# Gate products moved into the state-space groups, two multiplications left on GpSimd

## The chip, the cores and the metric

The kernel runs on one NeuronCore of one Trainium2 chip. The metric is the device time of one execution in microseconds, 2592.23 us in the median of three runs before the change (2590.69 to 2595.5).

## The reference, cut to what matters

The program is two transformer blocks in float32 on 256 tokens, the second with 256 more tokens of context. The change touches only the Mamba-2 mixer of the second block: 512 tokens (context and sequence, four tiles of 128), 8 groups of 4 heads, state size 128.

```python
z, xbc, dtr = split(u @ in_w)                 # z: 2048 gate columns = 16 chunks of 128
xbc = silu(dwconv(xbc) + b)                   # x (16 chunks of 128), B (8), C (8)
cb = einsum(C, B);  seg = exp(min(acum_l - acum_s, ...)) * tri
y_diag = einsum(cb * seg, x * dt)             # per group of 4 heads
y_off  = einsum(C, h_prev, exp(acum))
y = y_f + flip(y_b) + D * x
out = rmsnorm(y * silu(z), norm_w) @ out_w
```

## The kernel before

The mixer starts about 735 us into the execution and ends at 1318 us. Each engine has one instruction stream, written out in program order; a semaphore wait stops all that stands behind it on that engine. All activations are kept transposed, one chunk being 128 channels by 512 tokens.

**Weights** come in "halves" of 128 x 2048 (1 MB, two chunks of eight contraction tiles). Three slots hold raw halves, two hold the high parts. For each half ScalarE makes the high part (`round_half`, line 1768), VectorE the low part in place (`lower_half`, line 1773, which raises `w_split`), and TensorE multiplies three times for each pair of tiles (`matmul_split`, lines 464 to 466): 24 matmuls of 128x512 a chunk (`product`, line 1776). `product` waits for `w_split` to reach the number of its half, so it also waits for every half before it. The load of half w waits for half w-3 to be used, its rounding for half w-2. The order of halves before is 16 for x, B and C (two a group), 8 for z, 8 for the output projection.

**The group loop** runs over g = 0 to 7. TensorE in group g: chunk 0 of the next group; the C·B products and the transposes to token order (`to_tokens`, lines 1812 and 1818); chunks 1 and 2 of the next group; the states (line 1828); chunk 3; then `outputs` (line 1852), which waits for `m_ready` of both directions. Where there is no next group (g = 7), gate chunks 0 to 3 stand in those four places (`following`).

VectorE in group g: mask the C·B bank (line 2219), convolve chunk 0 of the next group (line 2114, four instructions), clip both directions of the decay rows (line 2230), mask_decay(0) (line 2236), convolve chunk 1, combine states (2249 to 2255), mask_decay(1), one `lower_half`, convolve chunks 2 and 3, add the output banks to `Yt` (line 2272), one more `lower_half`. ScalarE takes the banks out, makes the exponentials `cea` (lines 2068 to 2071, which release the clips) and the 32 decay exponentials (line 2007), and applies silu. GpSimd multiplies inputs by their weights (line 1960) and `cea` by C (line 1967); these are "the two multiplications" of the title, and they stay where they are.

**After the loop** TensorE makes gate chunks 4 to 15 (`gate`), with `sum_squares` of four chunks at a time (line 1906) between them, then the gate banks of `g1` (line 1688), the last sum and its transposition ("sst", line 1921), and the output projection: 8 halves of 48 matmuls of 128x512 into all eight PSUM banks. ScalarE applies silu to each gate bank (`gated`), squares (`square`) and rounds y; VectorE multiplies y by the gate (`use_gate`, line 2124) and makes the low part of y (`lower_y`, line 2129).

PSUM is a ring of eight banks in order of opening: a bank may be written when the one eight before it is emptied. After the mixer come the expert layers, whose weight loads wait for the last output bank.

## Time and profile before

| | |
|---|---|
| median of 3 runs | 2592.23 us (2590.69 to 2595.5) |
| the profiled execution | 2590.05 us |
| its span, first to last instruction | 2588.2 us (1.85 us lie around it) |
| TensorE / VectorE / ScalarE / GpSimd busy | 84% / 44% / 25% / 7% of the span |
| mean granted TensorE clock | 0.929 |
| mixer's group loop, first C·B mask to the end of the last outputs | 794.1 to 1147.9 us |
| after the loop, to the last matmul of the projection | 1147.9 to 1316.4 us |

Times are microseconds from the start of the span; "x8" is a count of instructions merged in one row, whose second number is then the time from the first's start to the last's end. "[3.33 <-PE bank L1812]" is idle time of the engine before the row, and what ended it. PE is TensorE, PEld its weight loads, DVE is VectorE, ACT is ScalarE, POOL is GpSimd. A clock of 1.00 is 2.4 GHz, 0.50 is 1.2 GHz.

### The profile page before, as it was taken

How to read it: one execution, taken by the hardware profiler on the slowest of the kernel's cores; microseconds unless marked ns; L12 is line 12 of the kernel's file. 1: busy time of each engine (PE TensorE's matmuls, PEld its weight loads, DVE VectorE, ACT ScalarE, POOL GpSimd, SP SyncE). 2: the span in 40 equal slices, each digit the busy share in tenths (PEclk: the TensorE clock that was granted, in tenths of full speed). 3: DMA queues.
4: the chain of work that ended last, by engine and by line, in shares of the span. 5: the costliest groups of instructions: out<-in, count | busy, mean ns of one | idle time of the engine just before them, and what ended most of it. 6: DMA issues, size and time to landing. Idle time of an engine off the chain costs nothing. (4 is left out here: it accounts for less than half of the span.)

```text
span 2588.2 us, 27436 instructions
## 1 busy us (share of the span) xinstructions
PE 2165.1 (84%) x10982; PEld 1296.4 (50%) x10982; DVE 1130.1 (44%) x1520; ACT 654.0 (25%) x1197; POOL 179.8 (7%) x103
## 2 busy tenths in 40 slices
PE   7975988999968868699968988888787879888886
PEld 5743455999957767577854322222343443222222
DVE  4566235777658888864141222212327421111112
ACT  4232132000036766654111111111104211111110
POOL 0000000000003524420000000000000000000000
PEclk9968988999979989899979999999898979999998
DMA  8735184555324223222243999999920129999997
GB/s 302 257 120 198 65 308 148 179 194 190 118 56 129 82 82 114 82 82 82 82 195 139 427 428 428 429 428 429 405 98 1 47 95 428 429 429 428 428 428 295
DMA packets 171348, 600.81 MB, mean 232 GB/s; under 512 B 14307, under 2 KB 97638, under 8 KB 144646
## 3 DMA queue, kind: packets, MB, share of 16 engines
q1 hardware_dynamic: 166640, 579.62, 57.2%
q0 software_dynamic: 2352, 16.91, 1.7%
q10 hardware_dynamic: 2278, 3.20, 0.4%
q8 instruction: 54, 0.88, 0.1%
q14 instruction: 24, 0.20, 0.0%
HBM read 598.53 MB, written 1.18 MB: 232 GB/s over the span
## 5 line engine op out<-in xcount | busy, mean ns | idle before, releaser
L2523 PE MATMUL bank<-slots,hT 128*64 128x512 f32 x3072 | 694.5, 599 | 119.9 <-DMA slots<-in_moe_w 87.2
L2523 PEld LDWEIGHTS bank<-slots,hT 128*64 128x64 f32 x3072 | 209.4, 137 | 558.9 <-issue 376.5
L464 PE MATMUL bank<-hT_r,slots_r 128*128 128x256 f32 (+1 forms) x896 | 299.0, 334 | 1.2 <-DVE slots_r L460 1.2
L2603 DVE TENSOR_TENSOR hT<-hT,bank 128x512 f32<-128x512 f32 x32 | 22.0, 688 | 527.0 <-PE bank L2523 527.0
L465 PE MATMUL bank<-slots_r 128*128 128x512 f32 x512 | 200.8, 392 | 0.0
L464 PEld LDWEIGHTS bank<-hT_r,slots_r 128*128 128x128 f32 x896 | 170.6, 190 | 20.9 <-issue 3.9
L330 POOL TENSOR_SCALAR rstd<-eps_rows 128x2 f32<-128x2 f32 (+4 forms) x16 | 3.9, 243 | 2145.8 <-ACT xn L396 683.1
L466 PE MATMUL bank<-slots_r 128*128 128x512 f32 x384 | 150.0, 391 | 0.0
L465 PE MATMUL bank<-hT_r,slots_r 128*128 128x256 f32 x512 | 144.8, 283 | 0.0
L466 PE MATMUL bank<-hT_r,slots_r 128*128 128x256 f32 x512 | 144.8, 283 | 0.0
L528 PE MATMUL bank<-slots,hT 128*128 128x512 f32 (+1 forms) x320 | 131.5, 572 | 4.0 <-ACT hT L445 2.7
L2584 ACT ACTIVATE hT<-bank 128x512 f32<-128x512 f32 x32 | 19.1, 597 | 450.5 <-PE bank L2523 450.5
L2114 DVE SCALAR_TENSOR_TENSOR slots<-slots,vcols 128x512 f32<-128x512 f32 x128 | 123.8, 972 | 13.4 <-ACT slots L1988 9.7
L2607 DVE TENSOR_TENSOR xne<-bank,xne 128x512 f32<-128x512 f32 x32 | 22.1, 692 | 222.6 <-PE bank L2523 222.6
L1852 PE MATMUL bank<-rowsB,slots 128*64 128x128 f32 x512 | 46.9, 341 | 78.7 <-DVE rowsB L2236 72.4
L460 DVE TENSOR_TENSOR slots_r<-slots,slots_r 128x4096 fp32r<-128x4096 f32 (+1 forms) x32 | 107.5, 3359 | 1.1
L465 PEld LDWEIGHTS bank<-slots_r 128*128 128x128 f32 x512 | 97.3, 190 | 19.5
L1967 POOL TENSOR_TENSOR slots<-slots 128x1536 f32<-128x1536 f32 (+2 forms) x24 | 105.8, 4432 | 0.0
L1773 DVE TENSOR_TENSOR slots_r<-slots,slots_r 128x2048 fp32r<-128x2048 f32 x32 | 73.2, 2287 | 69.7 <-ACT slots_r L1768 69.5
L2588 ACT ACTIVATE hT<-bank 128x512 f32<-128x512 f32 x32 | 19.1, 597 | 324.4 <-PE bank L2557 324.4
L465 PEld LDWEIGHTS bank<-hT_r,slots_r 128*128 128x128 f32 x512 | 98.1, 192 | 0.6
L466 PEld LDWEIGHTS bank<-hT_r,slots_r 128*128 128x128 f32 x512 | 98.1, 192 | 0.0
(457 smaller groups left out, 3299.2 us busy)
## 6 DMA issues: line engine op xcount, KB each, us to landing
slots<-in_moe_w SPq DMA_DIRECT2D x192, 2048.0 KB, 25.5
slots<-in_ada_w SPq DMA_DIRECT2D x24, 2048.0 KB, 11.6
slots<-in_ssd_in_w SPq DMA_DIRECT2D x48, 512.0 KB, 5.3
slots<-in_moe_w_gate SPq DMA_DIRECT2D x16, 1024.0 KB, 5.5
slots<-in_moe_w_up SPq DMA_DIRECT2D x16, 1024.0 KB, 8.0
slots<-in_moe_w_down SPq DMA_DIRECT2D x16, 1024.0 KB, 5.4
rowsB<-acum_rows POOLq DMA_DIRECT2D x16, 1024.0 KB, 6.4
slots<-in_w_in SPq DMA_DIRECT2D x7, 2048.0 KB, 17.9
```

Source lines behind the costliest of these rows:

```text
L460: return dve.tensor_tensor(low, x, high.bitcast(F32), ALU.subtract)
L464: pe.matmul(out, lhsT[0], rhs[1], start=start, stop=False, skip_group_check=True)
L465: pe.matmul(out, lhsT[0], rhs[0], start=False, stop=False, skip_group_check=True)
L466: return pe.matmul(out, lhsT[1], rhs[0], start=False, stop=stop, skip_group_check=True)
L528: i = pe.matmul(b.ap[:, 0:width], lhsT(k), rhs(k), start=(k == 0), stop=(k == K - 1))
L1773: dve.tensor_tensor(low_half(w), raw_half(w), high_half(w).bitcast(F32), ALU.subtract).then_inc(w_split, 1)
L1852: i = pe.matmul(pair[h // 2].ap[64 * j:64 * j + 64, tt], left, right, start=(at == 0), stop=(at == len(terms) - 1), tile_position=(0, 64 * ...
L1967: i = pool.tensor_tensor(cea[:, d, :, to:to + n], cea[:, d, :, to:to + n], conv[:, 3, at:at + n].unsqueeze(1).broadcast_to([P, HPG, n]), A ...
L2114: i = dve.scalar_tensor_tensor(o, padded[:, c, :, j:j + S], tap(j, CH(g)[c]), o, ALU.mult, ALU.add)
L2523: i = pe.matmul(bank[64 * n:64 * n + 64, :], lhsT(4 * h + k), wv[:, k, n * 512:(n + 1) * 512], start=(h == 0 and k == 0), stop=(h == 1 and ...
L2603: dve.tensor_tensor(acts, sg, psum[1][:, :], ALU.mult).then_inc(a_ready, 1)
L2607: dve.tensor_tensor(ye[j], psum[3][:, :], g2, ALU.mult).then_inc(ye_ready, 1)
```

## The change

Twelve of the sixteen gate chunks are made inside the groups. The order of halves becomes A0 B0 A1 B1, then A_g B_g Z_(g-2) for g = 2 to 7, then Z6 Z7 and the eight O (A: x, B: B and C, Z: gate, O: output projection). In groups 1 to 6 TensorE makes gate chunks 2g-2 and 2g-1 between chunk 3 and `outputs`; in group 7 the four places hold chunks 12 to 15; none is left after the loop. `sum_squares` takes two chunks at a time, and stands before `to_tokens` in groups 2 to 7 and twice after the loop. `round_half` and `lower_half` are called three times a group in the order of the halves; the clips now stand before the convolution of chunk 0. ScalarE and VectorE make silu, product and square of the two chunks in the same group. The high part of y is rounded after the loop, in the time of the projection; the transposition of the sums uses the last output bank. Buffers: gate values lie in the two last chunks of `Yt` until they are needed, `y_high` partly in `h_high`, `ssum` in `w_dt`. Nothing on GpSimd's queue changes. The diff, cut:

```diff
@@ -279,16 +279,17 @@
...
+        HALVES = [("A", 0), ("B", 0), ("A", 1), ("B", 1)]
+        for g in range(2, SSD_G):
+            HALVES += [("A", g), ("B", g), ("Z", g - 2)]
+        HALVES += [("Z", 6), ("Z", 7)] + [("O", q) for q in range(8)]
...
                         project(g + 1, c)
                     else:
-                        gate(c)
+                        gate(12 + c)
+
+                def sum_squares(q):
+
+                    pe.wait_ge(y_squared, 2 * q + 2)
+                    b = banks.open(("ss", q), DVE)
+                    pe.wait_ge(*b.emptied)
+                    for j in range(2):
+                        i = pe.matmul(b.ap[64 * j:64 * j + 64, :], const("ones")[:, 0:64], gate_buf(2 * q + j), start=True,
+                                      stop=True, tile_position=(0, 64 * j), skip_group_check=True)
...
@@ -1890,48 +1906,41 @@
                 project(0, 3)
                 for g in range(SSD_G):
                     following(g, 0)
+                    if g >= 2:
+                        sum_squares(g - 2)
                     to_tokens(g)
                     following(g, 1)
                     following(g, 2)
                     states(g)
                     following(g, 3)
+                    if 1 <= g < SSD_G - 1:
+                        gate(2 * g - 2)
+                        gate(2 * g - 1)
                     outputs(g)
 
-                def sum_squares(q):
-
...
@@ -2011,17 +2018,26 @@
 
                     b = banks["z", i]
                     act.wait_ge(bank_full, b.full)
-                    if i >= 2:
-                        act.wait_ge(z_used, i - 1)
-                    act.activation(sz[:, i % 2, :], b.ap[:, :], ACT.Silu).then_inc(emptied[ACTE], 1)
+                    if 2 <= i < 12:
+                        act.wait_ge(bank_full, banks["ss", i // 2 - 1].full)
+                    elif i >= 12:
+                        act.wait_ge(conv_done, 4 * SSD_G)
+                    act.activation(gate_buf(i), b.ap[:, :], ACT.Silu).then_inc(emptied[ACTE], 1)
 
                 def square(i):
 
                     act.wait_ge(z_used, i + 1)
-                    if i >= 4 and i % 4 == 0:
-                        act.wait_ge(bank_full, banks["ss", i // 4 - 1].full)
-                    act.activation(squares[:, i % 4, :], Yt[:, i, :], ACT.Square).then_inc(y_squared, 1)
-                    act.activation(y_high[:, i, :], Yt[:, i, :], ACT.Identity, scale=y_gain(i)).then_inc(y_rounded, 1)
+                    act.activation(gate_buf(i), Yt[:, i, :], ACT.Square).then_inc(y_squared, 1)
...
@@ -2054,52 +2070,66 @@
                     more = g + 1 < SSD_G
                     smooth(g, 3)
                     if more:
+                        if g:
+                            round_half(act, B_HALF(g + 1))
                         take(g + 1, 0)
                     else:
-                        gated(0)
+                        round_half(act, Z_HALF(7))
+                        gated(12)
                     for t in range(TT):
                         copy_out(act, ACTE, ("tok", g, t), tok[:, t, :], 384)
...
                     if more:
                         take(g + 1, 1)
                     decay(g, 1)
-                    if not more:
-                        gated(1)
-                    round_half(act, 2 * g + 4)
                     if more:
+                        if g:
+                            round_half(act, Z_HALF(g - 1))
                         smooth(g + 1, 0)
                         take(g + 1, 2)
                         smooth(g + 1, 1)
                         take(g + 1, 3)
+                        if g + 2 < SSD_G:
+                            round_half(act, A_HALF(g + 2))
+                        else:
+                            round_half(act, Z_HALF(6))
                         smooth(g + 1, 2)
+                        if g:
+                            for i in (2 * g - 2, 2 * g - 1):
+                                gated(i)
+                            for i in (2 * g - 2, 2 * g - 1):
+                                square(i)
                     else:
...
-                        gated(3)
-                    round_half(act, 2 * g + 5)
-                act.wait_ge(bank_full, banks["y", SSD_G - 1, 1].full)
-                for i in range(3):
-                    square(i)
-                for i in range(4, 16):
-                    gated(i)
-                    square(i - 1)
-                    if i % 2:
-                        round_half(act, 18 + i // 2)
+                        skip(g, 0)
...
                 square(15)
                 for s_ in range(2):
                     for n in range(2):
                         copy_out(act, ACTE, ("g1", s_, n), g1[:, s_, n * 512:(n + 1) * 512], 512)
-                for w in range(26, 32):
-                    round_half(act, w)
+                act.wait_ge(bank_full, banks["y", SSD_G - 1, 1].full)
+                for q in range(2, 8):
+                    round_y(2 * q - 2)
+                    round_y(2 * q - 1)
+                    round_half(act, OUT_HALF(q))
...
@@ -2219,28 +2284,20 @@
                         i = dve.tensor_tensor(cbm[:, d, :].rearrange("p (t n) -> p t n", t=TT),
                                               b.ap[:, :].rearrange("p (t n) -> p t n", t=TT), mask, ALU.mult)
                     i.then_inc(emptied[DVE], 1)
+                    if more and g:
+                        lower_half(dve, B_HALF(g + 1))
+                    elif not more:
+                        lower_half(dve, Z_HALF(7))
+                    clip(g, 0)
+                    clip(g, 1)
                     if more:
                         convolve(g + 1, 0)
...
-                        use_gate(0)
...
-                                          ALU.mult).then_inc(m_ready, 1)
-
-                    mask_decay(0)
+                        use_gate(12)
+                    dve.wait_ge(emptied[DVE], banks["cbs", g].done)
+                    mask_decay(g, 0)
                     if more:
...
@@ -2256,51 +2313,41 @@
                         i.then_inc(emptied[DVE], 1)
                         dve.wait_ge(emptied[DVE], b.done)
                     dve.sem_inc(hp_ready, 1)
-                    mask_decay(1)
-                    lower_half(dve, 2 * g + 4)
+                    mask_decay(g, 1)
                     if more:
+                        if g:
+                            lower_half(dve, Z_HALF(g - 1))
                         convolve(g + 1, 2)
+                        lower_half(dve, A_HALF(g + 2) if g + 2 < SSD_G else Z_HALF(6))
                         convolve(g + 1, 3)
+                        if g:
+                            use_gate(2 * g - 2)
+                            use_gate(2 * g - 1)
                     else:
-                        use_gate(2)
-                        use_gate(3)
-                    for c in range(2):
-                        b = banks["y", g, c]
-                        dve.wait_ge(bank_full, b.full)
...
+                        use_gate(13)
+                        lower_half(dve, OUT_HALF(0))
+                        lower_half(dve, OUT_HALF(1))
+                        lower_y(0)
+                        lower_y(1)
+                    add_output(g)
+                use_gate(14)
+                use_gate(15)
+                sum_batch(6)
+                sum_batch(7)
+                lower_y(2)
+                lower_y(3)
+                b = banks["so", TT - 1, 1]
+                dve.wait_ge(sst_full, 1)
+                dve.tensor_scalar(eps_rows[:, 0:TT], b.ap[:, 0:TT], 1.0 / 64, None, ALU.mult).then_inc(sst_taken, 1)
+                dve.wait_ge(sst_taken, 1)
+                dve.sem_inc(y_summed, 1)
+                for q in range(2, 8):
+                    lower_half(dve, OUT_HALF(q))
+                    if q < 7:
+                        lower_y(2 * q)
+                        lower_y(2 * q + 1)
                 lower_y(14)
                 lower_y(15)
-                sum_batch(3)
```

The helper `clip`, `mask_decay` and `add_output` hold the instructions of before; `skip` is the D·x product taken out of `smooth`.

## Rows read from the trace of the kernel before

**Rows 1.** Busy time by stretch: us, PE, PEld, DVE, ACT, POOL, clock, DMA.

```profile
950.00:1000.00 50.00, 36.70 (x247) 31.44 (x246) 44.47 (x37) 33.23 (x67) 20.99 (x9) 0.90 0.30 93
1150.00:1200.00 50.00, 50.00 (x227) 39.54 (x226) 23.74 (x25) 23.15 (x32) 0.00 (x0) 1.00 0.30 84
```

**Rows 2.** Costliest groups, page part 5: busy, mean ns, idle before, releaser.

```profile
L1852 PE MATMUL bank<-rowsB,slots 128*64 128x128 f32 x512 | 46.9, 341 | 78.7 <-DVE rowsB L2236 72.4
```

**Rows 3.** VectorE in group 4, in order of time: start, us, instruction.

```profile
976.83 1.29 DVE L2219 TENSOR_TENSOR slots<-bank,consts 128x512 f32<-128x512 f32 x2 [3.33 <-PE bank L1812]
979.49 5.04 DVE L2114 SCALAR_TENSOR_TENSOR slots<-slots,vcols 128x512 f32<-128x512 f32 x4 [1.37 <-ACT slots L1988]
984.45 8.20 DVE L2230 TENSOR_TENSOR rowsB<-rowsB,slots 128x2048 f32<-128x2048 f32 x2
992.57 3.38 DVE L2236 TENSOR_TENSOR rowsB<-rowsB,slots 128x2048 f32<-128x2048 f32 x1
995.88 5.22 DVE L2114 SCALAR_TENSOR_TENSOR slots<-slots,vcols 128x512 f32<-128x512 f32 x4
...
1004.88 2.29 DVE L2236 TENSOR_TENSOR rowsB<-rowsB,slots 128x2048 f32<-128x2048 f32 x1
1007.09 2.29 DVE L1773 TENSOR_TENSOR slots_r<-slots,slots_r 128x2048 fp32r<-128x2048 f32 x1
1009.29 6.13 DVE L2114 SCALAR_TENSOR_TENSOR slots<-slots,vcols 128x512 f32<-128x512 f32 x8
```

**Rows 4.** TensorE, outputs of group 3 and products of group 4.

```profile
961.93 1.97 PE L1852 MATMUL bank<-rowsB,slots 128*64 128x128 f32 x16 [10.34 <-DVE rowsB L2236]
...
970.12 0.50 PE L464 MATMUL bank<-hT_r,slots_r 128*128 128x512 f32 x1
...
975.74 1.05 PE L1812 MATMUL bank<-slots 128*128 128x128 f32 x8
...
977.86 0.48 PE L464 MATMUL bank<-hT_r,slots_r 128*128 128x512 f32 x1
...
988.84 2.75 PE L1828 MATMUL bank<-xst,slots 128*128 128x256 f32 x12
```

**Rows 5.** ScalarE in group 4, the exponential that releases the first clip.

```profile
982.29 1.50 ACT L2068 ACTIVATE slots<-rowsB 128x1536 f32<-128x1536 f32 x1
```

**Rows 6.** GpSimd in group 4, and its first product in group 7.

```profile
981.06 3.94 POOL L1960 TENSOR_TENSOR xst<-slots,wst 128x768 f32<-128x768 f32 x3 [9.45 <-ACT slots L541]
984.97 13.22 POOL L1967 TENSOR_TENSOR slots<-slots 128x1536 f32<-128x1536 f32 x3
...
1115.42 3.05 POOL L1960 TENSOR_TENSOR xst<-slots,wst 128x768 f32<-128x768 f32 x3 [7.22 <-ACT slots L541]
```

**Rows 7.** The clips of all groups: duration ns, min/median/max.

```profile
L2230 DVE TENSOR_TENSOR rowsB<-rowsB,slots x16: 2455/4132/5604, 801.6 to 1120.6; 128x2048 f32<-128x2048 f32 x16
```

**Rows 8.** TensorE busy and granted clock, in the outputs of group 3.

```profile
962.00:964.00 2.00, 2.00 (x20) 0.50 0.00 0
966.00:968.00 2.00, 2.00 (x41) 1.00 0.00 0
```

**Rows 9.** Group 7 and the stage after it, VectorE and TensorE.

```profile
1113.38 1.29 DVE L2219 TENSOR_TENSOR slots<-bank,consts 128x512 f32<-128x512 f32 x2 [3.30 <-PE bank L1812]
...
1132.93 0.69 DVE L2124 TENSOR_TENSOR Yt<-Yt,slots 128x512 f32<-128x512 f32 x1 [3.49 <-ACT slots L2016]
...
1146.87 1.06 PE L1852 MATMUL bank<-slots,hp 128*64 128x128 f32 x16
...
1158.96 1.07 PE L1906 MATMUL bank<-rowsB,consts 128*32 128x512 f32 x8
...
1216.95 3.73 PE L1688 MATMUL bank<-consts,modcol 128*128 128x128 f32 x32
...
1226.39 0.77 PE L464 MATMUL bank<-slots_r 128*128 128x512 f32 x1
...
1316.00 0.39 PE L466 MATMUL bank<-slots_r,Yt_r 128*128 128x512 f32 x1
```

More of the change, by code:

```diff
@@ L1794, in project @@
                 def project(g, c):
[L1795 removed]
+                    product((A_HALF, B_HALF)[c // 2](g), c % 2, ("ch", g, c), g == 0 and c == 0)
                 def gate(i):
[L1798 removed]
+                    product(Z_HALF(i // 2), i % 2, ("z", i), False)
                 def following(g, c):
@@ L1931, in _ @@
                             pe.wait_ge(*b.emptied)
+                        if q == 0 and (t, n) == (TT - 1, 1):
+                            pe.wait_ge(emptied[DVE], banks["ss", 7].done)
+                            for t_ in range(TT):
+                                i = pe.matmul(b.ap[:, t_:t_ + 1], ssum[:, t_ * P:(t_ + 1) * P], const("ones")[:, 0:1],
+                                              start=True, stop=True, skip_group_check=True)
+                            i.then_inc(sst_full, 1)
+                            pe.wait_ge(sst_taken, 1)
                         c = slice(n * 512, (n + 1) * 512)
                         for k in range(2):
-                            y = [a[:, 2 * q + k, t * P:(t + 1) * P] for a in (y_high, Yt_r)]
+                            y = [a[:, t * P:(t + 1) * P] for a in (y_high(2 * q + k), Yt_r[:, 2 * q + k, :])]
                             i = matmul_split(pe, b.ap[:, :], y, (wh[:, k, c], wl[:, k, c]), q == 0 and k == 0, q == 7 and k == 1)
@@ L2212, in _, with sum_batch, add_output, clip @@
                 lower_half(dve, 3)
+                def sum_batch(q):
+                    b = banks["ss", q]
+                    dve.wait_ge(bank_full, b.full)
+                    if q == 0:
+                        dve.tensor_copy(ssum, b.ap[:, :]).then_inc(emptied[DVE], 1)
+                    else:
+                        dve.wait_ge(emptied[DVE], banks["ss", q - 1].done)
+                        dve.tensor_tensor(ssum, ssum, b.ap[:, :], ALU.add).then_inc(emptied[DVE], 1)
+                def add_output(g):
+                    for c in range(2):
+                        b = banks["y", g, c]
+                        dve.wait_ge(bank_full, b.full)
+                        dve.wait_ge(skip_done, 2 * g + c + 1)
+                        y = Yt[:, 2 * g + c, :]
+                        dve.tensor_tensor(y, y, b.ap[:, :], ALU.add).then_inc(emptied[DVE], 1)
+                def clip(g, d):
+                    dve.wait_ge(ea_done, 2 * g + d + 1)
+                    r = rowsB[:, d, :, :].rearrange("p h (t n) -> p h t n", t=TT)
+                    a_s = acs[:, :, d * 32 + g * HPG:d * 32 + (g + 1) * HPG].rearrange("p t h -> p h t")
+                    dve.tensor_tensor(r, r, a_s.unsqueeze(3).broadcast_to([P, HPG, TT, P]), ALU.min).then_inc(clipped, 1)
+                def mask_decay(g, d):
+                    dve.wait_ge(exps_out, 2 * g + d + 1)
+                    r = rowsB[:, d, :, :]
+                    dve.tensor_tensor(r, r, cbm[:, d, :].unsqueeze(1).broadcast_to([P, HPG, TT * P]),
+                                      ALU.mult).then_inc(m_ready, 1)
                 for g in range(SSD_G):
                     more = g + 1 < SSD_G
+                    if g >= 2:
+                        sum_batch(g - 2)
                     b = banks["cbs", g]
@@ L2284, in _ @@
-                dve.wait_ge(emptied[DVE], banks["y", SSD_G - 1, 1].done)
-                lower_y(0)
-                lower_y(1)
-                for i in range(4, 16):
-                    use_gate(i)
-                    lower_y(i - 2)
-                    if i % 2:
-                        lower_half(dve, 18 + i // 2)
-                    if i % 4 == 2 and i > 4:
-                        sum_batch(i // 4 - 1)
+                        if g:
+                            use_gate(2 * g - 2)
+                            use_gate(2 * g - 1)
+                    else:
+                        use_gate(13)
[3 more added lines that the diff above has]
+                        lower_y(1)
@@ L2294, in _ @@
+                for q in range(2, 8):
[3 more added lines that the diff above has]
+                        lower_y(2 * q + 1)
                 lower_y(14)
                 lower_y(15)
-                sum_batch(3)
-                b = banks["sst"]
-                dve.wait_ge(bank_full, b.full)
-                dve.tensor_scalar(eps_rows[:, 0:TT], b.ap[:, 0:TT], 1.0 / 32, None, ALU.mult).then_inc(emptied[DVE], 1)
-                dve.wait_ge(emptied[DVE], b.done)
@@ L2301, in _ @@
-                dve.sem_inc(y_summed, 1)
-                for w in range(26, 32):
-                    lower_half(dve, w)
                 dve.wait_ge(y_rooted, 1)
```

122 lines of the change are left out of this document (48 added, 74 removed).

## The prediction

> **What bounds the kernel now.** I read the table of busy time by stretch first. In the group loop no engine is full: in 50 us VectorE works 44.47, TensorE 36.70, ScalarE 33.23 [rows 1]. After the loop TensorE works 50.00 of 50.00 at full clock [rows 1]. So a gate chunk costs its whole length after the loop, and the question is whether the loop has room for it. The list of the costliest groups says where TensorE idles: ahead of `outputs`, 72.4 us over the loop, released by mask_decay (line 2236) [rows 2]. The order of time gives the cycle of a group. Call X the moment VectorE begins to mask the C·B bank, and T the end of mask_decay(1).
>
> X to T is VectorE's: in group 4 from 976.83 to 1007.17, 30.3 us, of which it idles 1.37 [rows 3]. T to the next X is TensorE's: group 3's T lets `outputs` start at 961.93 after 10.34 us of idling; they end at 970.12, chunk 0 ends at 975.74, the C·B products at 976.8, and VectorE, which idled 3.33, starts its mask at 976.83 [rows 3, 4]: 15.1 us from T (about 961.7). The group is 45.4 us long, and both legs are on its path. What bounds the loop is this ring of VectorE's long leg and TensorE's short one, not the busy share of either.
>
> **The change part by part.**
>
> *The gate pair, on the path.* TensorE is idle for 10.34 us before `outputs`, and two gate chunks take 10.98 (two chunks run from 977.86 to 988.84 [rows 4]). They seem to fit. But `gate(2g-2)` waits for `w_split` of half Z_(g-1), and VectorE lowers that half only after mask_decay(g, 1), that is after T. So TensorE idles through the same wait, then waits 2.2 us more for the lowering (1007.09 to 1009.29 [rows 3]), then makes 10.98 us of gate products, and only then `outputs`, for which everything was ready at T. Queued behind the wait on TensorE are both gates, `outputs`, the next chunk 0 and the C·B products; for these VectorE waits. Each of groups 1 to 6 gets 2.2 + 11.0 = 13.2 us longer in its second leg: 6 x 13.2 = **+79.2 us**. VectorE's lowering can't be earlier than T by its own order, so neither end of this is soft.
>
> *sum_squares of two chunks*, in front of `to_tokens` in groups 2 to 7, on the same leg. Four column tiles took 1.07 us [rows 9]. Two wider ones are not in the trace: if they overlap as the four do it is 1.1, if they ran one after the other 2.1 at most. I take 1.1 (the same instruction), 6 x 1.1 = **+6.6 us**, up to +12.6.
>
> *The clips ahead of convolution 0, and lowering B.* Before, VectorE convolved chunk 0 while ScalarE made the exponentials that release the clips. Now it masks (1.3), lowers B (2.2), and has nothing to do until the first exponential ends at 982.29 + 1.50 = 983.79, X + 7.0 [rows 5]: 3.5 us idle, 5.7 in group 0, where B isn't lowered. What follows, alone: clips 2 x 2.46 (their shortest [rows 7]), convolutions 0 and 1 of 3.07 each (8 instructions in 6.13), mask_decay(0) and (1) of 2.2 each as the next start shows, states 3.8 (from 1001.1 to 1004.88) [rows 3]: 19.3. To that comes what GpSimd takes from VectorE. Before, convolution 0 took 5.04 where 3.07 is its time alone, the clips 8.20 where it is 4.9, mask_decay(0) 3.38 where it is 2.29, convolution 1 5.22 where it is 3.07 [rows 3, 7]: excesses of 2.0, 3.3, 1.1 and 2.2, 8.5 in all, all while GpSimd ran (981.06 to 998.2 [rows 6]). The first, 2.0, fell beside GpSimd's input products, which now run in VectorE's idle time, as they do in group 7 (3.05 us and not 3.94 [rows 6]). The other 6.6 fell beside its C products and stays, only on other instructions. X to T is then 7.0 + 19.3 + 6.6 = 32.9, or 32.4 with clips of 2.2 each; I take 32.7 against 30.3: +2.4 a group, groups 0 to 6, **+17 us**. Its ends are -33 (no excess at all) and +20.
>
> The Trainium skill, SBUF — State Buffer, section "Summary: rules for kernel authors", says that a VectorE instruction with two SBUF inputs and a GpSimd instruction that reads SBUF block each other, the second waiting for the first to finish. The clip's three kinds of duration (2455, 4132 in the median, 5604 ns [rows 7]) bear it out: one waits for a whole GpSimd instruction, one hardly. By the rule the excess is GpSimd's work and moves with it, so that the sum stays +17; without it the term would be -33.
>
> *Two more lowerings' places, use_gate, sum_batch.* The number of halves is unchanged (32); a third one a group (2.2 us) comes into VectorE's loop, and two use_gates and a sum_batch of 0.69 each [rows 9]. Z is counted above; A, the convolutions of chunks 2 and 3, and use_gate fall in the second leg, where VectorE has 29 us for about 13 us of work, so nothing. sum_batch lies between sum_squares and X. Without that cover they would cost 4.3 a group. ScalarE gets a round_half, two silus and two squares more, in the same leg; `smooth(g+1, 3)`, behind them in its queue, is late by some 8 us and is needed only before `to_tokens`, over 10 us later. The gate's bank is written when the token banks eight openings before are emptied, long since. The loads are the same 48 on SP's queue, each still three halves ahead; GpSimd's queue, with the row loads behind `outputs`, shifts as a whole. Nothing: 0.
>
> *Group 7.* VectorE waited 3.49 us for gate chunk 1 and spent 0.69 on it [rows 9]; now use_gate(12) alone lies in that leg: T comes some 3.5 us earlier. TensorE's last gate and `outputs` follow as before: **-3.5**, perhaps 1.5 more if the short idle leaves the clock up.
>
> *After the loop.* Before: the last outputs end at 1146.87 + 1.06 = 1147.9, the last matmul at 1316.4: 168.5 us [rows 9]. Of it remain sum_squares(6), the g1 banks (3.73), sum_squares(7), which has to wait for add_output(7), use_gate(15) and its square (about 5 us, under the first two), and the projection, 1226.39 to 1316.4, 90.0 us with its slow first 6 us. The transposition of the sums and its round trip to VectorE now lie inside that, 1 to 2 us. 1.1 + 3.7 + 1.1 + 90.0 + 1 = 96.9, so **-71.6 us**. Rounding and lowering y (four 0.7 us instructions) and a half take 3.5 to 4 us on each of the two engines for every 10.9 us of projection, hidden. All later stages shift as they are, since their loads wait for the last output bank.
>
> *Clock.* After the idle of 10.34 us `outputs` begin at half clock (0.50 at 962 to 964, 1.00 from 966 [rows 8]), some 4 us of it, 2 us lost. Now the gate pair starts slow in its place and `outputs` run at full clock. Even, if the slow stretch is no longer; 6 x 1.7 = +10 if it is twice as long after the longer idle.
>
> Sum: 79.2 + 6.6 + 17 - 3.5 - 71.6 = +27.7. Against the profiled execution, 2590.05, that is 2617.8; the median shown is 2.2 higher. I forecast **2618 us**, 1.0% slower.
>
> **The rivals.**
> (a) *More is lost on TensorE*: two column tiles run one after the other (+6) and the clock stays at half twice as long (+10): 2634. For it: the idle grows from 10.3 to some 14 us; against it: the same kind of restart is seen in every group already. 0.11.
> (b) *The pair fills the wait after all*, if TensorE gets Z's half before T: then 79.2 falls to about 6 x 2.2 for the lowering, and the sum to -38: 2552, faster. It decides from the place of the lowering: if it is done 11 us before T. Against: VectorE's order. It is also the reading on which the change would do what its shape suggests. 0.04.
> (c) *The reordering relieves VectorE from GpSimd* (-33 for +17): 2568, faster; the total becomes negative once X to T falls under 28.7 us, that is once under 2.4 of the 6.6 us of excess remain. Against: GpSimd's C products still start with the clips. 0.04.
> (d) *Half of each*: X to T is as before or shorter by a us or so, group 7 and the tail give 5 more: 2588 to 2597, no change. 0.05.
> Forecast, 2603 to 2631: 0.76.
>
> **How the numbers follow.** The forecast's own range holds the reordering at 0 to +20, the sums at 6.6 to 12.6, the clock at 0 to +10 in part, the tail at ±4: 2603 to 2631. With (a) 8 in 10 needs 2602 to 2633. A measurement here tells 0.2%, 5 us, from no change. Slower: 0.76 + 0.11 = 0.87; within: 0.05; faster: 0.08.
>
> **What would show it.** Right: in groups 1 to 6 the first matmul of line 466's kind after states and chunk 3 waits 13 to 15 us, released by the lowering (line 1773), not by line 2236; `outputs` wait for nothing; the mask of C·B waits some 14 us for TensorE; groups are 61 to 62 us apart (45.4 before); the clips wait 3.5 us for ScalarE; the loop ends some 97 us later and the mixer some 28 later. Wrong: if TensorE's gates start before T, (b) holds; if X to T is under 29 us, (c). If groups are 61 us apart and the total is unchanged, the tail was mis-sized.

## The result

The changed kernel takes 2617.52 us in the median of four runs (2613.93 to 2620.72), beside 2591.46 us for the kernel before on the same chip: a ratio of 1.0096, with a 95% interval of 1.008 to 1.0113. It is slower by 26 us. The forecast was 2618. The profiled execution took 2619.25 us, its span 2617.2.

Busy time of the changed kernel by stretch (us; PE, PEld, DVE, ACT, POOL; clock; DMA share and GB/s), most of one group in the loop and the stretch in which the projection begins, which answer to [rows 1]:

```profile
1000.00:1050.00 50.00, 47.31 (x292) 38.91 (x292) 30.67 (x25) 25.04 (x53) 15.80 (x8) 0.95 0.28 86
1250.00:1300.00 50.00, 49.75 (x230) 40.78 (x230) 13.17 (x15) 14.85 (x18) 1.27 (x2) 1.00 0.20 68
```

TensorE looks well used in the first stretch only because its 50 us hold less than one whole wait. The waits say more. Who waited for whom in the changed kernel, 840 to 1230 us: total, times, longest:

```profile
PEld bank L465 <- DVE slots_r L1779: 88.6, 6, 14.8
PE bank L465 <- DVE slots_r L1779: 86.1, 6, 14.4
...
DVE w_dt L2251 <- PE bank L1818: 28.0, 5, 5.6
```

TensorE's wait of 10.3 us for mask_decay [rows 4] has become one of 14.3 to 14.4 for the lowering of Z's half (line 1779 in the new numbering), six times: once in each of the groups 1 to 6. TensorE in group 3, at the gate's first matmul and at the first of `outputs`:

```profile
1000.84 0.79 PE L465 MATMUL bank<-hT_r,slots_r 128*128 128x512 f32 x1 [14.34 <-DVE slots_r L1779]
...
1013.78 1.09 PE L1868 MATMUL bank<-rowsB,slots 128*64 128x128 f32 x16
```

The gate pair (the two gate chunks of one group) lies between 1000.84 and 1013.78; `outputs` follow it with no wait at all. VectorE in group 4 of the changed kernel, which answers to [rows 3]:

```profile
1027.91 1.29 DVE L2284 TENSOR_TENSOR slots<-bank,consts 128x512 f32<-128x512 f32 x2 [0.39 <-PE bank L1828]
1029.12 2.28 DVE L1779 TENSOR_TENSOR slots_r<-slots,slots_r 128x2048 fp32r<-128x2048 f32 x1
1034.89 7.96 DVE L2267 TENSOR_TENSOR rowsB<-rowsB,slots 128x2048 f32<-128x2048 f32 x2 [3.50 <-ACT slots L2084]
1042.77 6.16 DVE L2144 SCALAR_TENSOR_TENSOR slots<-slots,vcols 128x512 f32<-128x512 f32 x4
1048.85 2.28 DVE L2273 TENSOR_TENSOR rowsB<-rowsB,slots 128x2048 f32<-128x2048 f32 x1
...
1057.93 2.29 DVE L2273 TENSOR_TENSOR rowsB<-rowsB,slots 128x2048 f32<-128x2048 f32 x1
1060.14 2.28 DVE L1779 TENSOR_TENSOR slots_r<-slots,slots_r 128x2048 fp32r<-128x2048 f32 x1
...
1089.46 1.29 DVE L2284 TENSOR_TENSOR slots<-bank,consts 128x512 f32<-128x512 f32 x2 [0.39 <-PE bank L1828]
```

X (VectorE begins to mask the C·B bank) is 1027.91, T (the end of mask_decay(1)) is 1060.2, the next X 1089.46. The first leg is 32.3 us (before 30.3), the second 29.2 (before 15.1), the group 61.55 (before about 45.4). The 3.50 us in front of the clips are the wait for ScalarE's exponential.

Where the time went, from X of group 0 on:

| stretch | before | after | difference | forecast |
|---|---|---|---|---|
| X of group 0 to X of group 7 | 319.3 | 417.0 | +97.8 | +102.8 |
| X of group 7 to the end of its outputs | 34.5 | 34.7 | +0.1 | -3.5 |
| to the last matmul of the projection | 168.5 | 95.5 | -73.0 | -71.6 |
| the mixer | | | +24.9 | +27.7 |

The spans of the two profiled executions differ by 29.0; the 4 us that are left lie ahead of the first X and behind the mixer, where nothing was changed. The medians differ by 26.1.

### The profile page after: what moved, and what is told of

It is laid out like the page before. It is cut to its first block and busy times, and to the rows that moved or that the text cites. A ratio compares the mean times of both kernels' runs of the same rounds, so it can differ in the third digit from the quotient of the medians.

```text
span 2617.2 us, 27445 instructions
## 1 busy us (share of the span) xinstructions
PE 2169.0 (83%) x10982; PEld 1290.5 (49%) x10982; DVE 1118.4 (43%) x1524; ACT 654.3 (25%) x1197; POOL 164.5 (6%) x103
## 5 line engine op out<-in xcount | busy, mean ns | idle before, releaser
L465 PE MATMUL bank<-hT_r,slots_r 128*128 128x256 f32 (+1 forms) x896 | 304.4, 340 | 87.2 <-DVE slots_r L1779 86.1
L466 PE MATMUL bank<-slots_r 128*128 128x512 f32 x512 | 204.8, 400 | 0.0
L467 PE MATMUL bank<-slots_r 128*128 128x512 f32 x384 | 153.9, 401 | 0.0
L2144 DVE SCALAR_TENSOR_TENSOR slots<-slots,vcols 128x512 f32<-128x512 f32 x128 | 117.5, 918 | 3.9 <-ACT slots L1997 0.2
L529 PEld LDWEIGHTS bank<-slots,hT 128*128 128x128 f32 x320 | 60.5, 190 | 72.8 <-issue 67.0
L1976 POOL TENSOR_TENSOR slots<-slots 128x1536 f32<-128x1536 f32 (+2 forms) x24 | 93.2, 3912 | 0.0
L1779 DVE TENSOR_TENSOR slots_r<-slots,slots_r 128x2048 fp32r<-128x2048 f32 x32 | 73.1, 2285 | 41.7 <-ACT slots_r L1774 41.5
```

The lines of the kernel that those rows point to most:

```text
L465: pe.matmul(out, lhsT[0], rhs[1], start=start, stop=False, skip_group_check=True)
L466: pe.matmul(out, lhsT[0], rhs[0], start=False, stop=False, skip_group_check=True)
L467: return pe.matmul(out, lhsT[1], rhs[0], start=False, stop=stop, skip_group_check=True)
L529: i = pe.matmul(b.ap[:, 0:width], lhsT(k), rhs(k), start=(k == 0), stop=(k == K - 1))
L1779: dve.tensor_tensor(low_half(w), raw_half(w), high_half(w).bitcast(F32), ALU.subtract).then_inc(w_split, 1)
L1976: i = pool.tensor_tensor(cea[:, d, :, to:to + n], cea[:, d, :, to:to + n], conv[:, 3, at:at + n].unsqueeze(1).broadcast_to([P, HPG, n]), A ...
```

## The experiments

All ratios are to the kernel before, run beside each on the same chip. The kernels e4, e5, e6, e9 and e11 leave out or add part of the computation, as their texts say; the others compute the whole.

### Z lowered 2.2 us earlier (e1_z_before_mask1)

```diff
-                    mask_decay(g, 1)
-                    if more:
-                        if g:
-                            lower_half(dve, Z_HALF(g - 1))
+                    if more and g:
+                        lower_half(dve, Z_HALF(g - 1))
+                    mask_decay(g, 1)
+                    if more:
```

> The kernel after the change, with one step moved: VectorE lowers the gate half Z just before mask_decay(1) and not just behind it; T (end of mask_decay(1)) comes 2.2 us later, the gate products 2.2 us earlier. Theory (the gates' start hangs on the lowering, and outputs hang on the gates): each of groups 1 to 6 is 2.2 us shorter, 6 x 2.2 = 13 us, 2604 us, 1.005 of the kernel before. Rival (the loop is held by VectorE's total work, whose order does not matter): 2617 us as after the change.

Measured: 2602.57 us (2600.48 to 2605.41), ratio 1.0047 (1.0033 to 1.0062), 15 us less than the changed kernel. VectorE does the same work in another order, and the time follows the moment of the lowering. From X of group 0 to X of group 7 it needs 405.6 us against 417.0, 11.5 less where 13 were worked out.

### Z rounded early and lowered behind the clips (e2_z_after_clips)

```diff
@@ scalar
+                    if more and g:
+                        round_half(act, Z_HALF(g - 1))
                     decay(g, 0)
...
-                        if g:
-                            round_half(act, Z_HALF(g - 1))
@@ vector
                     clip(g, 1)
+                    if more and g:
+                        lower_half(dve, Z_HALF(g - 1))
...
                     mask_decay(g, 1)
                     if more:
-                        if g:
-                            lower_half(dve, Z_HALF(g - 1))
```

> The kernel after the change, with Z's rounding moved ahead of the decay exponentials on ScalarE and its lowering on VectorE to right behind the clips, some 15 us after X. Theory: TensorE finds Z's half ready when chunk 3 is done (X + 20), makes the gate pair while VectorE is on its way to T, and outputs start at T. First leg 32.3 + 2.2 = 34.5, second leg back to 15.1 + 1.1 = 16.2: 50.7 us a group against 61.5, 6 x 10.8 = 65 us less, 2552 us, 0.985. Rival (the gate pair costs its whole 11 us wherever it stands, for TensorE or VectorE is full): 2617 us, or 2604 if only the lowering's 2.2 us are won.

Measured: 2546.27 us (2539.0 to 2549.32), ratio 0.9833 (0.9813 to 0.9852): 71 us less, and 44 less than the kernel before. The place of one half's preparation turns the change from a loss into a gain. Both engines' orders were changed for it: in the changed kernel ScalarE rounds this half in group 4 until 1049.7, 7 us after the clips end (1042.8), so VectorE could have lowered it there only by waiting. Either move alone was not run. TensorE, first matmuls of `outputs` in groups 1 and 2 of this kernel:

```profile
872.53 1.09 PE L1868 MATMUL bank<-rowsB,slots 128*64 128x128 f32 x16 [3.85 <-issue]
921.60 1.86 PE L1868 MATMUL bank<-rowsB,slots 128*64 128x128 f32 x16 [3.80 <-issue]
```

The wait ahead of `outputs` is 3.8 us (before 10.3 [rows 4]): the pair has filled the rest, and also the 4.4 us by which the first leg is longer than before (34.7 against 30.3). The groups are 49.1 or 50.7 us long, and the two rows show 1.09 and 1.86 us for the same 16 matmuls; the clock is taken up below, with e9.

### Convolution 0 ahead of the clips again (e3_conv_first)

```diff
-                    clip(g, 0)
-                    clip(g, 1)
                     if more:
                         convolve(g + 1, 0)
                     else:
                         use_gate(12)
+                    clip(g, 0)
+                    clip(g, 1)
```

> The kernel after the change, with convolution 0 ahead of the clips again, as before the change. Theory (the reordering leaves VectorE idle for 3.5 us, 5.7 in group 0, until ScalarE's exponential, and saves 2 us of contention): the first leg goes from 32.3 to about 31.1, in group 0 to 30.3: 6 x 1.2 + 2 = 9 us less, 2608 us. Rival (the new order is the better one, since the GpSimd input products run free): 2617 us or more.

Measured: 2610.18 us (2608.47 to 2613.38), ratio 1.0079 (1.006 to 1.0098). The median is 7 us under that of the changed kernel, but the two intervals overlap, so the times alone don't settle it; the traces do, in part. VectorE in group 4:

```profile
1027.36 5.32 DVE L2144 SCALAR_TENSOR_TENSOR slots<-slots,vcols 128x512 f32<-128x512 f32 x4
1032.60 8.88 DVE L2267 TENSOR_TENSOR rowsB<-rowsB,slots 128x2048 f32<-128x2048 f32 x2
1043.12 2.77 DVE L2273 TENSOR_TENSOR rowsB<-rowsB,slots 128x2048 f32<-128x2048 f32 x1 [1.64 <-ACT rowsB L2014]
```

The 3.50 us of waiting ahead of the clips are gone, more contention is there again, and a new wait of 1.64 us has come: mask_decay(0) now waits for ScalarE's decay exponentials. The first leg is 31.0 us (1023.95 to 1054.98) against 32.3, and 30.2 against 32.2 in group 0: 9.8 us less in seven groups, where 9 were worked out. But from X of group 0 to X of group 7 only 5.0 are won. In groups 3 to 6 the second leg is 30.1 to 30.4 us and not 29.2 to 29.3, because the gate pair takes 13.7 to 14.0 us and not 12.8 to 12.9. In group 5 TensorE starts the pair at 1118.50 and its clock is still at half here:

```profile
1122.00:1124.00 2.00, 2.00 (x6) 0.50 0.00 0
1124.00:1126.00 2.00, 2.00 (x9) 0.86 0.00 0
```

That is some 6 us of half clock after the restart. In group 5 of the changed kernel the pair starts at 1124.04 and the clock is at 1.00 from 1128 on, after less than 4.

### The C products left out (e4_no_c_products)

```diff
-                        for at, to, n in runs:
-                            i = pool.tensor_tensor(cea[:, d, :, to:to + n], cea[:, d, :, to:to + n], ...
-                        i.then_inc(cea_ready, 1)
+                        pool.sem_inc(cea_ready, 1)
```

> The kernel after the change; GpSimd's three multiplications of the exponentials by C in each group are left out (cea goes to the outputs unmultiplied), everything else and every wait stays. Theory (6.1 us of VectorE's first leg are waits for GpSimd's C products): first leg from 32.3 to 26.2 us in groups 0 to 6, 43 us less, and 2 to 4 us in group 7: 2572 us, 0.993; each clip takes 2.2 to 2.5 us, no convolution instruction over 0.8. Rival (the excess is VectorE's own, or comes from ScalarE and DMA traffic): 2617 us, durations as they were.

Measured: 2565.37 us (2562.42 to 2571.37), ratio 0.9904 (0.988 to 0.9928), 52 us less than the changed kernel. VectorE in group 4:

```profile
1011.54 4.65 DVE L2264 TENSOR_TENSOR rowsB<-rowsB,slots 128x2048 f32<-128x2048 f32 x2 [3.50 <-ACT slots L2081]
1016.11 3.10 DVE L2141 SCALAR_TENSOR_TENSOR slots<-slots,vcols 128x512 f32<-128x512 f32 x4
```

The clips take 4.65 us and not 7.96, convolution 0 takes 3.10 and not 6.16: 6.4 us less, which is the excess that the prediction carried over to the new order (6.6). From X of group 0 to X of group 7 this kernel needs 375.5 us against 417.0: 41.5 of the forecast 43. So the C products, one of the two multiplications on GpSimd, cost VectorE some 6 us a group, on the path. The input products, the other one, are still in this kernel. The first leg of group 7 is 4.1 us shorter (21.3 against 25.3).

### Half of each gate product left out (e5_half_gates)

```diff
-                    for k in range(KD):
+                    K = KD // 2 if tag[0] == "z" and tag[1] < 12 else KD
+                    for k in range(K):
...
```

> The kernel after the change, but gate chunks 0 to 11 use only four of their eight contraction tiles (12 matmuls and not 24; the other half of the products is left out). Theory (the gate pair lies with its whole length on the path of groups 1 to 6): 12 x 12 matmuls x 0.227 us = 33 us less, 2585 us, 0.998. Rival (the pair is covered in part by the wait for mask_decay): less than 15 us won, 2603 us or more.

Measured: 2580.72 us (2576.33 to 2585.7), ratio 0.9956 (0.9943 to 0.9969), 37 us less than the changed kernel, where 33 were worked out. The spans of the traces differ by 33.3 us, 30.5 of it between X of group 0 and X of group 7. The pair lies on the path in its whole length.

### The same, with Z lowered early (e6_early_half_gates)

The edits of the second and the fifth experiment together.

> The kernel with Z lowered behind the clips (2546 us), with the same half of the products of gate chunks 0 to 11 left out. Theory (there the pair lies wholly in the time in which TensorE waits for VectorE): nothing is won, 2546 us, or up to 12 us lost (2558 us) if the longer idle puts the first matmuls of outputs at half clock, 2 us a group. Rival (the pair is still on the path in part): up to 33 us less, 2513 us.

Measured: 2549.28 us (2547.49 to 2552.26), ratio 0.9839 (0.9822 to 0.9856), beside 2546.27 and 0.9833 with the whole products. Twelve times twelve matmuls less, 33 us of TensorE's work, and no gain. TensorE in group 1:

```profile
878.66 1.98 PE L1869 MATMUL bank<-rowsB,slots 128*64 128x128 f32 x16 [9.29 <-issue]
```

It waits 9.2 to 9.3 us in all six groups where it waited 3.8 with the whole products: the 5.5 us taken out have become waiting. A gain hidden by a slower clock is no rival here: the first legs are the same 34.7 us, and `outputs` start 0.2 us after T in both. The clock costs something too: it is at half at the start of `outputs` in all six groups, whose second legs are 16.5 to 16.7 us, against 14.4 or 16.0 with the whole products. These two runs together show the main step of the prediction: the same work costs its full length behind T and nothing ahead of it.

### Both moves (e7_both_moves)

The edits of the second and the third experiment together.

> The kernel with Z lowered behind the clips (2546 us), and convolution 0 ahead of the clips again. Theory (the two act on different stretches of VectorE's first leg and add): the 7 us that the second one gave alone come on top, 2539 us, 0.980. Rival (with Z's lowering in the leg, VectorE has no idle left that the old order could fill): 2546 us.

Measured: 2528.53 us (2526.36 to 2532.49), ratio 0.9766 (0.9747 to 0.9785), 18 us less than the second experiment and not 7. It is the fastest kernel of this study, 89 us under the changed kernel and 63 under the one before. VectorE in group 4, and TensorE's first matmuls of `outputs` there:

```profile
1001.84 4.48 DVE L1779 TENSOR_TENSOR slots_r<-slots,slots_r 128x2048 fp32r<-128x2048 f32 x1
1006.25 2.28 DVE L2273 TENSOR_TENSOR rowsB<-rowsB,slots 128x2048 f32<-128x2048 f32 x1
```

```profile
1017.84 1.09 PE L1868 MATMUL bank<-rowsB,slots 128*64 128x128 f32 x16 [0.27 <-issue]
```

Two things come together. The first is the gain of the other order, 1.5 us on the first leg (33.2 us against 34.7) where it was 1.3 alone. Z's lowering fills the 1.64 us in which mask_decay(0) waited for ScalarE in the third experiment, but it takes 4.48 us there beside GpSimd's products (3.38 in the second experiment, 2.28 alone), so little of that is won. The second is the clock. VectorE reaches T so early that TensorE hardly stops ahead of `outputs` (0.2 to 0.3 us), and the granted clock stays at 1.00 through them in all six groups. The second leg is 14.4 us in each; in the second experiment it was 16.0 in the four groups where the clock fell. From X of group 0 to X of group 7 this gives 6 times 1.5, 4 times 1.7 and 1 us in group 0, near the 16.4 us by which the stretch is shorter. The expectation had only the first.

### Work added to keep the clock (e9_early_longer_gates)

```diff
-                    for k in range(KD):
+                    K = KD + 2 if tag[0] == "z" and tag[1] < 12 else KD
+                    for n in range(K):
+                        k = n % KD
...
```

> The kernel with Z lowered behind the clips (2546 us), and work added: gate chunks 0 to 11 use ten contraction tiles and not eight (tiles 0 and 1 twice, so their sums are others), 6 matmuls or 1.4 us more a chunk. Theory (in the kernel without it TensorE idles 3.8 us ahead of outputs and then runs them at half clock for 3.4 us, 1.6 us lost; with 2.7 us of that idle filled the clock stays up): the six groups of 49.1 to 50.7 us become 49.1 at most, about 6 to 8 us less in all, 2539 us, and outputs' first 16 matmuls take 1.09 us in every group. Rival (the gain of both moves over the sum of each had another cause): 2546 us, or more with the added work.

Measured: 2537.43 us (2532.16 to 2539.8), ratio 0.9804 (0.9788 to 0.982), beside 2546.27 and 0.9833 without the added work. The medians are 9 us apart, 7.5 if each is taken beside its own kernel before. But the intervals of the ratios overlap a little (the second experiment's begins at 0.9813), so here too the traces decide: all six groups take 49.1 us, where four of the second experiment's six took 50.7; X of group 1 to X of group 7 is 294.4 us against 301.1. The clock in group 4 of the second experiment (us, PE busy, clock, DMA share, GB/s):

```profile
1020.00:1022.00 2.00, 0.00 (x0) 1.00 0.72 187
1022.00:1024.00 2.00, 0.93 (x17) 1.00 1.17 313
1024.00:1026.00 2.00, 2.00 (x26) 0.54 0.11 25
1026.00:1028.00 2.00, 2.00 (x26) 0.61 0.02 4
1028.00:1032.00 4.00, 4.00 (x61) 1.00 0.02 4
```

TensorE idles 3.8 us until 1023.1, and the clock is at half for part of the `outputs` that follow. Their first row shows 1.09 us even so, because the clock falls only behind it; the length of the second leg tells the two kinds of group apart. With the added work the idle is 1.1 us in every group, and the clock stays at 1.00 through `outputs` in all six, as it does with both moves. Group 2 of this kernel, just behind the idle:

```profile
924.00:928.00 4.00, 4.00 (x78) 1.00 0.62 161
```

The Trainium skill says in TensorE: Matmul & The Clock Gate, section "What's actually happening", that the clock falls to half after idling and comes back under work; these rows agree.

### The sums moved off the second leg (e8_sums_behind)

`sum_squares(g - 2)` stands behind `to_tokens(g)`, and `sum_batch(g - 2)` behind the C·B mask; the rest as with both moves.

> The kernel with both moves, and sum_squares and sum_batch put behind to_tokens and the C.B mask, off the way from T to X. Theory (sum_squares is 1.1 us on the second leg in groups 2 to 7): 6 x 1.1 = 6.6 us less than with both moves, 2532 us, 0.977. Rival (it costs as much in the first leg, on VectorE, as it gave): 2539 us.

Measured: 2530.62 us (2525.99 to 2535.22), ratio 0.977 (0.9747 to 0.9793): the same as with both moves (2528.53). VectorE in group 4:

```profile
985.12 1.29 DVE L2282 TENSOR_TENSOR slots<-bank,consts 128x512 f32<-128x512 f32 x2 [3.77 <-PE bank L1828]
987.45 0.69 DVE L2251 TENSOR_TENSOR w_dt<-w_dt,bank 128x512 f32<-128x512 f32 x1 [1.04 <-PE bank L1818]
988.06 2.29 DVE L1779 TENSOR_TENSOR slots_r<-slots,slots_r 128x2048 fp32r<-128x2048 f32 x1
990.26 8.36 DVE L2144 SCALAR_TENSOR_TENSOR slots<-slots,vcols 128x512 f32<-128x512 f32 x4
```

The rival's account was right, no gain over both moves, though its number was not: both texts counted from an expected 2539 us, so the theory's 2532 is nearer by luck. sum_batch waits 1.04 us for TensorE and takes 0.69 on VectorE's first leg, which is now 34.7 us and not 33.2 (group 2: 888.17 to 922.85). The second leg is 13.2 us there and not 14.4: what was won on one leg is paid on the other. In groups 3 and 4 the second leg is 14.4 again, and the mask behind it waits 3.8 us and not 2.5. The trace shows why. TensorE in group 3, with the clock from 961 on:

```profile
959.46 0.50 PE L465 MATMUL bank<-hT_r,slots_r 128*128 128x512 f32 x1 [1.98 <-DVE slots_r L1779]
961.00:965.00 4.00, 4.00 (x12) 0.58 0.46 116
972.19 1.09 PE L1868 MATMUL bank<-rowsB,slots 128*64 128x128 f32 x16
```

TensorE waits 1.98 us for Z's lowering, and then runs part of the gate pair at half clock. The pair ends after T (970.7), and `outputs` start 1.5 us late. Groups 2, 5 and 6 have the same wait of 1.98 us and no fall of the clock.

### The clips first, in the kernel before (e10_before_clips_first)

```diff
-                    if more:
-                        convolve(g + 1, 0)
-                    else:
-                        use_gate(0)
                     for d in range(2):
                         dve.wait_ge(ea_done, 2 * g + d + 1)
...
+                    if more:
+                        convolve(g + 1, 0)
+                    else:
+                        use_gate(0)
```

> The kernel before the change, with the clips ahead of convolution 0 and nothing else. Theory (VectorE then waits 5.7 us for ScalarE's exponential in every group, and only the 1.4 us wait for the bank and 2 us of contention go): first leg 30.3 to about 32.3 us, 7 x 2 = 14 us more, 2605 us, 1.0055. Rival (the new order is neutral, the 3.5 us idle in the changed kernel comes from something else): 2591 us.

Measured: 2604.76 us (2603.02 to 2610.11) beside 2587.85, ratio 1.0059 (1.0039 to 1.0078), 17 us slower. VectorE in group 4:

```profile
988.93 1.29 DVE L2219 TENSOR_TENSOR slots<-bank,consts 128x512 f32<-128x512 f32 x2 [3.32 <-PE bank L1812]
995.92 7.96 DVE L2226 TENSOR_TENSOR rowsB<-rowsB,slots 128x2048 f32<-128x2048 f32 x2 [5.70 <-ACT slots L2068]
```

The clip starts 7.0 us after X, as worked out from [rows 5], and the first leg is 32.3 us, 2.0 more than before. This is the reordering's term alone: 14 us on the first legs of groups 0 to 6, and some 2 on their second legs (X of group 0 to X of group 7 is 16.3 us longer).

### The C products left out of the kernel before (e11_before_no_c_products)

The same edit as in the fourth experiment.

> The kernel before the change; GpSimd's multiplications of the exponentials by C are left out. Theory (6.6 us of VectorE's first leg are waits for them, but then ScalarE's first decay exponentials, done at X + 14.6, are next in line): first leg 30.3 to about 26 us, 7 x 4.3 = 30 us less, 2561 us, 0.988. Rival (the contention is only there in the new order): 2591 us; and if nothing else comes due, 46 us less, 2545 us.

Measured: 2561.76 us (2559.77 to 2563.11) beside 2587.85, ratio 0.9894 (0.9874 to 0.9913), 26 us less. VectorE in group 5:

```profile
1007.62 4.90 DVE L2227 TENSOR_TENSOR rowsB<-rowsB,slots 128x2048 f32<-128x2048 f32 x2
1015.25 2.29 DVE L2233 TENSOR_TENSOR rowsB<-rowsB,slots 128x2048 f32<-128x2048 f32 x1 [2.73 <-ACT rowsB L2004]
```

The contention was there before the change too. But in the old order its removal is partly lost on a wait of 2.73 us for ScalarE's decay exponentials; in the new order, where the clips come first, all of it is won: the first leg shrinks by 3.7 us here (30.3 to 26.6) and by 6.4 there (32.3 to 26.0).

## Why the prediction was right

**The gate pair** was the term that decided, and it came as forecast: TensorE waited for the lowering and not for mask_decay, 14.3 to 14.4 us each time (13 to 15 forecast), and `outputs` waited for nothing. With the sums, the second leg of groups 1 to 6 grew by 14.1 us where 14.3 had been worked out. One of the signs came otherwise: the mask of C·B was to wait some 14 us for TensorE, and it waits 0.39. VectorE does idle 15.5 us in group 3's second leg, but most of it lies ahead of the second use_gate (4.75, for ScalarE), the adding of the output banks (4.74) and sum_batch (5.61), which stand in front of the mask in its queue. The experiments e5 and e6 show that this is a matter of place: 33 us of gate work taken away give 37 us behind T and nothing ahead of it. Rival (b), the faster outcome, failed only because of where Z's half stood in the queues of ScalarE and VectorE; with rounding and lowering moved it is real, and was measured at 2546 us against the 2552 worked out for it.

**sum_squares of two chunks**: the four records of the pair took 1.08 us, so two wider column tiles overlap as four narrow ones do (1.07 [rows 9]). The low end held.

**The clips first** cost 2.0 us in the first leg and not 2.4: 14 us and not 17. The wait of 3.50 us was as worked out, and the contention 6.1 to 6.4 us where 6.6 was carried over. e10 gives the term alone as +17, where 14 was expected; e3 takes 7 us of it back. Rival (c), that the contention would go, is refuted by the first leg itself, 32.3 us and not under 28.7. e4 shows whose contention it is: without GpSimd's C products it is gone, and 52 us with it.

Which instruction of VectorE stands beside the products changes from kernel to kernel, and each time that one is long: the clips (7.96 us, 4.65 without the products), convolution 0 (6.16 and 3.10), Z's lowering in e7 (4.48 and 2.28), use_gate(12) below (3.97 and 0.69). The Trainium skill's rule in SBUF — State Buffer, section "Summary: rules for kernel authors", that a two-input instruction of VectorE and a GpSimd instruction that reads SBUF block each other, agrees with these rows. The excess beside the C products is 6.1 to 6.6 us a group, in the changed kernel and in the one before. GpSimd's own time for the C products is about 6.1 us, an estimate: in group 4 of the changed kernel its input products, half as many elements a row, take 3.05 us where VectorE idles beside them.

Two things of the prediction's working on this term don't come out. Its "three kinds of duration" of the clips [rows 7] are the least, the median and the greatest of sixteen, and there are only two kinds: eight clips of 2.5 to 2.7 us and eight of 5.6, between which the median of 4.13 lies. And a reordering with no excess at all is (2.4 - 6.6) x 7 = -29 by its own numbers and not -33, which would put rival (c) at 2572 us. The forecast hangs on neither.

**Group 7** is the step that failed: T was to come 3.5 us earlier, and the stretch came out 0.1 longer. GpSimd and VectorE there, before the change:

```profile
1118.44 13.25 POOL L1967 TENSOR_TENSOR slots<-slots 128x1536 f32<-128x1536 f32 x3
```

```profile
1118.17 7.98 DVE L2230 TENSOR_TENSOR rowsB<-rowsB,slots 128x2048 f32<-128x2048 f32 x2 [2.91 <-ACT slots L2068]
1126.08 3.35 DVE L2236 TENSOR_TENSOR rowsB<-rowsB,slots 128x2048 f32<-128x2048 f32 x1
```

And after it:

```profile
1220.88 11.64 POOL L1976 TENSOR_TENSOR slots<-slots 128x1536 f32<-128x1536 f32 x3
```

```profile
1217.27 5.80 DVE L2267 TENSOR_TENSOR rowsB<-rowsB,slots 128x2048 f32<-128x2048 f32 x2 [1.32 <-ACT slots L2084]
1222.99 3.97 DVE L2154 TENSOR_TENSOR Yt<-Yt,slots 128x512 f32<-128x512 f32 x1
1226.88 3.38 DVE L2273 TENSOR_TENSOR rowsB<-rowsB,slots 128x2048 f32<-128x2048 f32 x1
...
1230.90 2.25 DVE L2310 TENSOR_TENSOR hp<-hp,decs 128x256 f32<-128x256 f32 x2
```

The use_gate that was moved in between, 0.69 us alone, takes 3.97, and the first pair of state products, 0.76 together where undisturbed, takes 2.25: both stand beside GpSimd's products. Before, VectorE waited for ScalarE from 1129.4 to 1132.9 [rows 9], and GpSimd's products ran on in that wait until 1131.7. The wait that was removed had been a cover for GpSimd: 2.5 of its 3.5 us came back as contention, and the first leg is only 1.0 us shorter (25.3 against 26.3). What the prediction applied to the clips it did not apply to this instruction. The last microsecond went on TensorE's clock: `outputs` took 9.1 us and not 8.0, with 1.95 us for their second set of 16 matmuls where it had been 1.51.

**After the loop**: -73.0 where -71.6 was worked out. The projection took 90.0 us again, but not in the same way: its first matmuls ran at full clock (0.50 and 0.39 us where it had been 0.77 and 0.63), and later ones stood 0.70 us apart by threes where it had been 0.68, which takes the gain back. Why they stand further apart was not followed up.

**Clock**: even, as taken. TensorE's restart at half clock fell into the gate pair (0.79 and 0.63 us for its first matmuls) and `outputs` ran at full clock. Rival (a), with a slow stretch twice as long, did not occur, though e3 shows one in group 5.

**The total** is better than its parts, and that is luck. The errors of +3.6 in group 7, -5.0 in the loop and -1.4 after it leave the mixer 2.8 us under the forecast of +27.7. Outside it, where the forecast had nothing, the profiled executions differ by 4 us more, and the medians, 26.1 us apart, by about 1.

## What to carry to other kernels

An idle stretch of an engine is room only for work whose inputs are there when it begins: before moving work into it, find the last thing that this work waits for, and look where that stands in the queue of the engine that makes it. Here the wait's end and the new work's release came from the same queue, one behind the other, and moving one `lower_half` and its `round_half` was worth 71 us, 2.7%. Where GpSimd and VectorE both read from SBUF, a wait of VectorE may be what hides GpSimd's work, so that removing it wins nothing.

## What the runs showed of the hardware that was not expected

More work made the kernel faster: 16 us of matmuls added to the second experiment's gate chunks (12 times 6 at 0.227 us) took about 9 us off its median. TensorE's pause ahead of `outputs` became shorter by them, and its clock stayed at 2.4 GHz. The 6.7 us that the loop gained in the trace are the four groups in which the clock had fallen, at 1.7 us each; the rest of the medians' 9 us is within what they scatter.

The runs side by side: in the group loop every pause of TensorE of 4.9 us and more brought half clock (group 7 of twelve of the thirteen kernels has one of 4.9 to 6.3 us). The pause of 3.8 us did so in four of the second experiment's six groups. The pause of 1.98 us ahead of e8's gate pair did so in two of the five groups that have it. One of 2.66 us ahead of the projection in the kernel before brought it too (0.50 from 1226 on). The pauses of 1.7 to 1.8 us ahead of the pair in e7, and those of 1.1 us in e9 and 0.2 to 0.3 in e7 ahead of `outputs`, brought it in no group. What decides within the 3.8 and the 1.98 us was not tried.
